# A 512-point position transform with its tables standing in TensorE and 512 data columns moving

## The reference

```python
h = rmsnorm(x, ln_mix_g)
z = h @ w_in                              # 384 + 256 + 32 + 512 columns
c_q, c_kv, k_rope, u = split(z)
q  = rmsnorm(c_q, q_norm_g) @ w_uq        # 8 heads, 64 + 32 rotary
kv = rmsnorm(c_kv, kv_norm_g) @ w_ukv
A  = softmax(q @ k.T * scale) @ v         # with the rotary key k_rope
f  = fftn(u.reshape(512, 4, 128), axes=(position, channel), norm='ortho').real
B  = einsum('sgc,gcd->sgd', f, w_fnet)
x += concat(A, B) @ w_out                 # then memory attention and SwiGLU
```

## Time and profile before

| | us |
|---|---|
| median of 3 runs (1427.02 to 1427.57) | 1427.05 |
| the profiled execution | 1423.45 |
| its span, first to last instruction | 1421.7 |
| PE busy | 1381.4 (97%) |
| DVE, ACT, POOL busy | 810.4, 656.9, 834.7 |
| chain that ended last: PE | 39% of the span |

### The profile page before, as it was taken

The page is one execution under the profiler, slowest core; times in us unless marked ns, Lnnn a source line. Parts: engine busy times, 40 slices in busy tenths (PEclk is TensorE's granted clock), DMA queues, the critical chain, the costliest instruction groups (busy, mean ns, idle before and its releaser), DMA issues. The chain is left out here.

```text
span 1421.7 us, 18322 instructions
## 1 busy us (share of the span) xinstructions
PE 1381.4 (97%) x6696; PEld 1159.3 (82%) x6696; DVE 810.4 (57%) x999; ACT 656.9 (46%) x1207; POOL 834.7 (59%) x631
## 2 busy tenths in 40 slices
PE   8999999999999999999999899999999999999998
PEld 6977779888889787888887688888888888878776
DVE  3576643134445574431645876666656664488966
ACT  5567635445335664553544533333323323444355
POOL 4648857741446677595246665555545554477884
PEclk9999999999999999999999999999999999999999
DMA  8401044513323101463144043332333325973234
GB/s 277 166 23 38 23 149 134 166 49 127 99 66 93 38 16 52 149 186 120 50 126 172 30 141 111 112 106 88 110 112 112 111 82 199 311 237 115 79 103 156
DMA packets 99145, 164.66 MB, mean 116 GB/s; under 512 B 8560, under 2 KB 40688, under 8 KB 99056
## 3 DMA queue, kind: packets, MB, share of 16 engines
q1 hardware_dynamic: 99056, 163.48, 35.1%
HBM read 134.88 MB, written 28.57 MB: 115 GB/s over the span
## 5 line engine op out<-in xcount | busy, mean ns | idle before, releaser
L749 POOL TENSOR_TENSOR w_lo<-w_raw,w_hi 128x512 fp32r<-128x512 f32 (+2 forms) x236 | 307.0, 1314 | 228.7 <-ACT w_hi L904 227.8
L1909 PE MATMUL ps<-h_hi_P,w_hi 128*128 128x512 f32 x616 | 241.2, 392 | 5.8 <-DVE h_lo_P L1350 3.1
L1910 PE MATMUL ps<-h_lo_P,w_hi 128*128 128x512 f32 x616 | 240.4, 390 | 0.0
L1911 PE MATMUL ps<-h_hi_P,w_lo 128*128 128x512 f32 x616 | 240.3, 390 | 0.0
L904 ACT ACTIVATE w_hi<-w_raw 128x512 fp32r<-128x512 f32 (+2 forms) x236 | 140.9, 608 | 197.0 <-PE ps L1911 180.8
L749 POOL TENSOR_TENSOR w_lo<-w_sum,w_hi 128x512 fp32r<-128x512 f32 x88 | 118.4, 1349 | 115.9 <-ACT w_hi L904 115.9
L749 POOL TENSOR_TENSOR w_lo<-a_raw,w_hi 128x512 fp32r<-128x512 f32 x77 | 111.9, 1455 | 74.2 <-ACT w_hi L904 74.1
L1909 PEld LDWEIGHTS ps<-h_hi_P,w_hi 128*128 128x128 f32 x616 | 116.0, 188 | 32.5 <-issue 4.7
L1909 PE MATMUL ps<-w_hi,act_hi 128*128 128x512 f32 (+2 forms) x384 | 140.6, 366 | 1.5 <-POOL w_lo L749 1.5
L1911 PE MATMUL ps<-w_hi,act_lo 128*128 128x512 f32 (+2 forms) x384 | 139.8, 364 | 0.0
L1910 PE MATMUL ps<-w_lo,act_hi 128*128 128x512 f32 (+2 forms) x384 | 139.8, 364 | 0.0
(11 more groups left out here) (242 smaller groups left out, 3046.1 us busy)
## 6 DMA issues: line engine op xcount, KB each, us to landing
gu_raw<-in_w_gate_up SPq DMA_DIRECT2D x22, 1024.0 KB, 5.5
a_raw<-a_mem SPq DMA_DIRECT2D x77, 256.0 KB, 2.7
w_raw<-in_w_xkv SPq DMA_DIRECT2D x64, 256.0 KB, 3.2
a_mem<-down_sum SPq DMA_DIRECT2D x44, 256.0 KB, 2.6
wd<-in_w_down SPq DMA_DIRECT2D x44, 256.0 KB, 5.6
a_mem<-act_t SPq DMA_DIRECT2D x33, 256.0 KB, 2.1
w_raw<-in_w_out SPq DMA_DIRECT2D x32, 256.0 KB, 2.6
w_raw<-in_w_xq SPq DMA_DIRECT2D x32, 256.0 KB, 2.9
```

What stands on the lines that cost most here:

```text
L749: return nc.gpsimd.tensor_tensor(out, whole, hi.bitcast(F32), ALU.subtract)
L1909: nc.tensor.matmul(out, s_hi, m_hi, start=start, stop=False, skip_group_check=more)
L1910: nc.tensor.matmul(out, s_hi, m_lo, start=False, stop=False, skip_group_check=more)
L1911: return nc.tensor.matmul(out, s_lo, m_hi, start=False, stop=stop, skip_group_check=more)
```

## The change

The position transform is turned round. `fourier_class(k)` lets a table stand (dft_hi, dft_lo) and moves f of all four channel groups, 512 columns, past it: 4 classes x 2 parts x 3 passes = 24 products in all. Its result has positions down and channels across, in the four banks that z1 has left (FY_BANK). ACT copies each to a tile y_f in SBUF, and `fourier_positions(c)` is now four transposes of y_f for each channel group (16 in all), into tenancies that come after the latents. The latents are parted: "cq" (3 tenancies, query latents) is transposed ahead of the classes, "ck" (2, key-value latents) behind them. PE, ACT, DVE and POOL take their parts in a new order, and some tiles lie at other addresses.

```diff
-             ("positions", FG, None), ("c", CQ + CK, None),
+             ("cq", CQ, None), ("ck", CK, None), ("positions", FG, None),
...
+        y_f = at("y_f", R + 64, [P, ROOT, FG * P])
...
+        FY_BANK = [(TEN["z1"] + k) % BANKS for k in range(ROOT)]
...
-                pool.wait_ge(psum_full.sem, psum_full.at(g, FA[FG - 1] + 2))
+                rotate_key(g)
+                pool.wait_ge(fy_full.sem, fy_full.at(g, ROOT))
                 nc.gpsimd.memset(v_hi_st[:, :, :, 1, :].bitcast(F32), 1.0).then_inc(v_filled.sem, 1)
                 nc.gpsimd.memset(v_lo_st[:, :, :, 1, :].bitcast(F32), 0.0).then_inc(v_filled.sem, 1)
-                rotate_key(g)
...
+                for f in range(CQ):
+                    hi_out(g, TEN["cq"] + f, c_hi[:, f, :], bank(TEN["cq"] + f))
                 act.wait_ge(psum_free.sem, psum_free.at(g, TEN["z1"] + T))
                 for t in range(T):
                     square(g, T + t, z[:, t, QR:QR + KR], c_junk[:, 0:KR], t, KR)
                 root(g, 2 * T, 0, T)
+                for k in range(ROOT):
+                    act.wait_ge(fy_full.sem, fy_full.at(g, k + 1))
+                    copy(y_f[:, k, :], ps[:, FY_BANK[k], :]).then_inc(fy_copied.sem, 1)
+                for f in range(CK):
+                    hi_out(g, TEN["ck"] + f, c_hi[:, CQ + f, :], bank(TEN["ck"] + f))
                 for c in range(FG):
                     fourier_out(c)
-                for f in range(CQ + CK):
-                    hi_out(g, TEN["c"] + f, c_hi[:, f, :], bank(TEN["c"] + f))
...
+                for f in range(CQ):
+                    lo_out(g, HI["cq"] + f, TEN["cq"] + f, c_lo[:, f, :], bank(TEN["cq"] + f), c_hi[:, f, :])
                 invert(g, 1, T)
                 for t in range(T):
                     a = z[:, t, QR:QR + KR]
                     normed(a, a, t, c_gain[:, QR:QR + KR]).then_inc(c_normed.sem, 1)
-                fourier_out(0)
-                fourier_out(1)
-                fourier_out(2)
-                fourier_out(3)
-                for f in range(CQ + CK):
-                    lo_out(g, HI["c"] + f, TEN["c"] + f, c_lo[:, f, :], bank(TEN["c"] + f), c_hi[:, f, :])
+                for f in range(CK):
+                    lo_out(g, HI["ck"] + f, TEN["ck"] + f, c_lo[:, CQ + f, :], bank(TEN["ck"] + f), c_hi[:, CQ + f, :])
+                for c in range(FG):
+                    fourier_out(c)
...
+                def fourier_class(k):
+                    pe.wait_ge(psum_free.sem, psum_free.at(g, TEN["z1"] + k + 1))
+                    out = ps[:, FY_BANK[k], :].rearrange("p (c d) -> p c d", c=FG)
+                    for a in range(2):
+                        last = three(out, dft_hi[:, a, k, :], dft_lo[:, a, k, :], f_hi[:, :, k, a, :], f_lo[:, :, k, a, :],
+                                     a == 0, a == 1)
+                    last.then_inc(fy_full.sem, 1)
+
                 def fourier_positions(c):
...
+                    claim(g, FB[c])
                     for k in range(ROOT):
...
+                        last = nc.tensor.transpose(ps[:, FB[c] % BANKS, K1[k] * P:(K1[k] + 1) * P],
+                                                   y_f[:, k, c * P:(c + 1) * P], ident[:])
+                    last.then_inc(psum_full.sem, 1)
...
-                for c in range(FG):
-                    fourier_positions(c)
-
+                pe.wait_ge(c_normed.sem, c_normed.at(g, T))
+                for f in range(CQ):
+                    latent("cq", 0, f)
+                pe.wait_ge(dft_ready, 1)
+                pe.wait_ge(f_ready.sem, f_ready.at(g, FG))
+                for k in range(ROOT):
+                    fourier_class(k)
                 pe.wait_ge(c_normed.sem, c_normed.at(g, 2 * T))
...
+                for f in range(CK):
+                    if f >= 1:
+                        pe.wait_ge(fy_copied.sem, fy_copied.at(g, f))
+                    latent("ck", CQ, f)
...
                 key_rope(g)
+                pe.wait_ge(fy_copied.sem, fy_copied.at(g, ROOT))
+                for c in range(FG):
+                    fourier_positions(c)
```

More of the change, by code:

```diff
@@ L236, in build @@
         o1 = at("o1", R + 68, [P, 2, P])
+        y_f = at("y_f", R + 64, [P, ROOT, FG * P])
         z = at("z", R + 76, [P, T, ZW])
         c_gain = at("c_gain", R + 86.5, [P, QR + KR])
-        c_hi = at("c_hi", R + 44, [P, CQ + CK, S], F32R)
-        c_lo = at("c_lo", R + 54, [P, CQ + CK, S], F32R)
+        c_hi = at("c_hi", R + 6, [P, CQ + CK, S], F32R)
+        c_lo = at("c_lo", R + 16, [P, CQ + CK, S], F32R)
         k_rot = at("k_rot", R + 72, [P, 4, T, HALF])
@@ L246, in build @@
         q_f = at("q_f", R + 4, [P, S])
-        v_hi_st = at("v_hi_st", R + 6, [P, T, PAIRS, 3, DV], F32R)
-        v_lo_st = at("v_lo_st", R + 18, [P, T, PAIRS, 3, DV], F32R)
+        v_hi_st = at("v_hi_st", R + 32, [P, T, PAIRS, 3, DV], F32R)
+        v_lo_st = at("v_lo_st", R + 44, [P, T, PAIRS, 3, DV], F32R)
         y_raw = at("y_raw", R + 30, [P, S])
-        kt_hi = at("kt_hi", R + 32, [P, 2, S], F32R)
-        kt_lo = at("kt_lo", R + 36, [P, 2, S], F32R)
-        prob = at("prob", R + 40, [P, 2, S])
+        kt_hi = at("kt_hi", R + 26, [P, 2, S], F32R)
+        kt_lo = at("kt_lo", R + 56, [P, 2, S], F32R)
+        prob = at("prob", R + 60, [P, 2, S])
         qt_hi = at("qt_hi", R + 64, [P, 2, S], F32R)
@@ L446, in build @@
         n = 0
-        for name, count in (("chan01", 2), ("chan23", 2), ("positions", FG), ("c", CQ + CK),
+        for name, count in (("chan01", 2), ("chan23", 2), ("cq", CQ), ("ck", CK), ("positions", FG),
                             ("vv", T), ("mem", 2 * MT), ("xk0", 4), ("n2t0", 2), ("xk1", 4), ("n2t1", 2), ("xv0", MT),
@@ L2134, in fourier_channels, with latent @@
                         last.then_inc(psum_full.sem, 1)
-                def fourier_positions(c):
[L2137 to L2142, removed]
-                    for k in range(ROOT):
[L2144 to L2147, removed]
+                def fourier_class(k):
[5 more added lines that the diff above has]
+                    last.then_inc(fy_full.sem, 1)
+                def fourier_positions(c):
+                    claim(g, FB[c])
+                    for k in range(ROOT):
+                        last = nc.tensor.transpose(ps[:, FB[c] % BANKS, K1[k] * P:(K1[k] + 1) * P],
+                                                   y_f[:, k, c * P:(c + 1) * P], ident[:])
+                    last.then_inc(psum_full.sem, 1)
+                def latent(name, first, f):
+                    claim(g, TEN[name] + f)
+                    for t in range(T):
+                        last = nc.tensor.transpose(ps[:, (TEN[name] + f) % BANKS, t * P:(t + 1) * P],
+                                                   z[:, t, (first + f) * P:(first + f + 1) * P], ident[:])
                     last.then_inc(psum_full.sem, 1)
@@ L2154, in _ @@
                                                               5: lambda: fourier_channels(3)})
-                for c in range(FG):
-                    fourier_positions(c)
-                pe.wait_ge(c_normed.sem, c_normed.at(g, 2 * T))
-                for f in range(CQ + CK):
-                    claim(g, TEN["c"] + f)
-                    for t in range(T):
-                        last = nc.tensor.transpose(ps[:, (TEN["c"] + f) % BANKS, t * P:(t + 1) * P],
-                                                   z[:, t, f * P:(f + 1) * P], ident[:])
-                    last.then_inc(psum_full.sem, 1)
+                pe.wait_ge(c_normed.sem, c_normed.at(g, T))
[5 more added lines that the diff above has]
+                    fourier_class(k)
+                pe.wait_ge(c_normed.sem, c_normed.at(g, 2 * T))
+                for f in range(CK):
+                    if f >= 1:
+                        pe.wait_ge(fy_copied.sem, fy_copied.at(g, f))
+                    latent("ck", CQ, f)
                 def out0(k):
```

12 lines of the change are left out of this document (8 added, 4 removed).

## The result

The changed kernel takes 1429.15 us in the median of 20 runs (1427.14 to 1433.58), the kernel before 1426.41 in 20 runs of the same chip (1424.12 to 1429.79). The ratio is 1.0023, with a 95% interval of 1.0017 to 1.0029: slower by 0.2%, a small step, but one whose interval leaves out no change. The forecast was 1429.1, its likeliest case one clock drop. The number holds; the case behind it, as the rows show, does not.

A forecast was written before the change was run, and what follows sets the result against it. TensorE, 97% busy, was taken as the bound. Saved work and old waits against new waits gave +0.2 in two groups, one clock drop +1.9, on 1427.05: 1429.15, rounded to 1429.1 us; range 1426.7 to 1431.2.

The forecast's parts named there:

- The work: PE, position transform: 96 narrow products (10.75 us) become 24 wide (5.5) plus 16 transposes (1.8), saving 3.45 per group.
- The first wait: PE before the query latents' transposes: stands still about 4.8 us per group until DVE has normed the four token tiles.
- The chain behind it: From query latents' transposes to first query product: only 0.1 us of wait; row maxima 0.05 later, rounded to 0.1 per group.
- The last wait: PE at the row maxima: a new pause of 1.45 us per group, waiting for DVE's kt_lo behind the four act_lo.
- The clock, how often: After the 4.8 us pauses in two groups: one drop to half speed taken as likeliest for the median, chance 0.38.
- The clock, its price: Classes behind the pause: 3.95 us of them at half speed, +2.0 per drop, 1.9 reaching the end; bounds nothing and 2.6.
- 1.9 leaves the clock up: Old wait at the first query product: after a 1.9 us pause the 512-column pitch is 0.23 at once, full clock.
- The base: Starting time: median 1427.05 us, 3.6 above the profiled execution's 1423.45; both moved by the same amounts.
- Drops in both groups: Rival: the clock falls after the 4.8 us pause in each group; 1431.0 us, slower; chance 0.22.
- Clock holds: Rival: the clock stays up through the 4.8 us pauses ahead of the query latents; 1427.3 us; chance 0.30.
- Drains keep up: Rival: DVE and ACT finish q_f and kt_lo early, row maxima at 87.6, saving 1.4 per group; 1424.2 us; chance 0.05.
- Slow feed: Rival: 512-column products fed in four pieces run slower, classes up to 10.8 us, not 5.5; up to 1437; chance 0.03.

The follow-up runs named there:

- fillers: The changed kernel with 20 unused 512-column matmuls on TensorE between the last z1 product and the wait for the normed query latents: 1427.41 us, ratio 1.0000.

## Why the prediction was right, and where it was wrong

- **The work.** Right. 0.112 became 0.228 for four times the columns, fed in pieces, and the transposes of y_f cost 1.7, where 1.8 was forecast. The rule of the Trainium skill weighed there ("TensorE: Matmul & The Clock Gate", Phases on the wall clock: 56 ns at 128 columns) is not what these float32 products show.
- **The first wait.** Right: 4.8 forecast, 4.80 and 4.78 measured.
- **The chain behind it.** Right: no wait at the key-value latents or the first query product; ACT's y_f copies and DVE's early c_lo lie beside the classes. With the clock up the chain gives 21.4 (fillers, less the longer norm) against 21.46 before; forecast was 0.1 more.
- **The last wait.** Right: 1.45 forecast, 1.40 and 1.38 measured, on kt_lo.
- **The clock, how often.** Wrong. One drop was taken as likeliest (0.38), both drops had 0.22. Both groups drop in both traces of the change. The step that failed is "may differ from group to group": for a pause of 4.8 it doesn't, in any trace here. The clock mean was 0.992 to 0.994 in 19 of 20 runs and in 12 of 12, which fits; but a mean doesn't say where the clock fell, and in the variant with the rotary key split first, with the same pauses, three of ten runs had 0.996 or 0.997. So two drops in every run is not shown.
- **The clock, its price.** Right by luck in part: 2.0 per drop forecast, 2.8, 2.6, 1.6 and 2.2 measured in the two traces of the change (against the fillers), 2.3 on average. The transposes behind the pause, which the step took as free, run at half pace too and cost 1.1 to 1.2; the classes cost 0.5 to 1.6 instead of 2.0. The upper bound, 12 x 0.21, is 2.5 and not 2.6, and was passed in two of four. (The pace at the start was read from the pitch, 0.44. The granted clock of the profile says 1.00 there; where it says 0.50, as behind the new pause, the pitch is 0.43.)
- **"1.9 leaves the clock up."** Wrong as a rule. It was read from one place of one execution. The second trace of before loses the clock behind the same wait, and the first one itself, read further on, behind 1.86 at 809.62. So the claim that "no row of a mid-kernel pause" shows a price of the clock was true of the rows listed, not of the trace.
- **The base.** Two errors cancelled here, and the hit to 0.05 us is luck. The forecast rise was 2.1 on a base of 1427.05, the median of three runs; twenty runs of the kernel before gave 1426.41, so the base was 0.6 too high and the rise, measured as 2.7, 0.6 too small. Two drops alone, at 1.6 to 2.8 each, would make the rise 3.8 to 5.4. Between the first traces it is 5.3, because the profiled execution of before, 1423.45, was faster than each of those twenty (1424.12 at least) and had no drop around the transforms; between the second traces it is 1.7. The step "the median lies 3.6 above it, and I move it by the same amounts" took what lies between that execution and the median as untouched by the change. Part of it is clock lost behind waits that the change removes: 1.3 of the 2.6 us between the two traces of before. The rest of the 2.6 lies in other stretches (0.5 between the groups, 0.7 behind the row maxima of group 1) and is not explained, and how much clock the median run of before loses around its transforms is not shown.
- **The rivals.** Drops in both groups: the mechanism is the one in the traces, its 1431.0 is 1.9 too high for the reason just given. Clock holds: true only with fillers. Drains keep up: no, act_lo took 4.00. Slow feed: no, 0.23 at full clock.

The Trainium skill ("TensorE: Matmul & The Clock Gate", HAM oscillation) spoke against the change, and the traces agree: each pause of 4.1 to 4.8 that was read was followed by the lower clock.

## What to carry to other kernels

When a change swaps many narrow products for few wide ones, the saving can be read from the pitches; read as carefully what the new order makes PE wait for, since here pauses of 6.2 us per group and their clock paid the whole of it back. Before turning a product, look at the order on the engine that drains it: six lines moved on DVE were worth about twice what the turned transform was. And take a second trace of the kernel before, when its waits are near the size that is argued about, and read the granted clock over the whole of the first: one execution can show the clock up in a stretch where others lose it.

## What the runs showed of the hardware that was not expected

- 96 products of 128 columns ran 20.5 us at 1.2 GHz (granted clock 0.50) without a gap, at a pitch of 0.213. The clock came back only in the transposes behind them, while the turned transform had it back 3.6 to 6.0 us after its pause. In one of two groups the clock fell about 1.2 us behind a pause of 1.41.
- The clock also fell where no wait was longer than 1.92: behind 0.58 and 1.92 with 24 transposes between them (one of two groups), and behind 0.7 to 0.8 four times and 1.86, at 810 us of the first trace of before.
- Four norms of 128x384 on DVE took 4.25 to 4.37 or 5.38 to 5.47, and between the change and the fillers nothing in DVE's program differed. Single ones took 0.60 to 0.68 or 1.61 to 1.73. Norm and POOL's f_lo both read their operands from SBUF. The long single ones had a subtraction of POOL's (f_lo, w_lo) beside them for nearly all of their time, the short ones only the end of one, or they started just ahead of it. In the change the second norm starts 0.04 ahead of f_lo: it takes 0.60 and f_lo 1.69. With fillers it starts 0.03 ahead by the rows: it takes 1.73 and f_lo 1.29. That looks as if one waits for the other and a tie decides which, but no run tested it, and the rows are too coarse to show who came first. The long form came where 512-column products started right behind z1 (fillers, and the classes in the version with classes first); what shifts the tie there is open. With fillers it made PE's wait 1.2 us longer per group.
